# A two-block transformer kernel on one core: B first, square sums folded, low parts in their own turn, GpSimd held back at nine stage starts

## What is computed

```python
def rms_norm(x, g):
    y = x * lax.rsqrt(jnp.mean(x * x, axis=-1, keepdims=True) + EPS)
    return y * g
...
    h = rms_norm(x, ssm_norm)                       # layer 0
    x = x + s5_mixer(h, ...)                        # state space: u = h @ w_in, complex scan, gelu, @ w_glu
    x = x + conv_ffn(rms_norm(x, ffn_norm), ...)
    x = x + sigmoid(rms_norm(x, ple_norm) @ w_gate) * (p @ w_proj)
    k, v = shared_kv(x, ...)                        # rms_norm(x, kv_norm) @ kv_w, then norms of k
    x = x + diff_attention(rms_norm(x, attn_norm), k, v, ...)
    ...                                             # conv_ffn and the gate again
    x = x + even_mixer(rms_norm(x, g0), ...)        # attention over selected keys, pooled windows
    x = x + swiglu(rms_norm(x, g1), w1, w3, w2)
    x = x + odd_mixer(rms_norm(x, g2), ...)         # stick-breaking attention
    x = x + swiglu(rms_norm(x, g3), w1, w3, w2)
```

## Time and profile before

| | us |
|---|---|
| median of 3 runs | 1413.98 (1412.37 to 1414.03) |
| the profiled execution | 1413.15 |
| its span, first to last instruction | 1411.4 |

### The profile page before, as it was taken

How to read it: one execution, slowest core, us unless ns; L and a number is a source line. 1 busy time by engine, 2 the same in 40 slices (tenths; PEclk the granted TensorE clock), 3 DMA queues, 4 the chain that set the end, 5 groups by cost and what they waited for, 6 DMA issues and landing times.

```text
span 1411.4 us, 28128 instructions
## 1 busy us (share of the span) xinstructions
PE 1343.0 (95%) x11090; PEld 1295.0 (92%) x11090; DVE 688.7 (49%) x1174; ACT 687.4 (49%) x961; POOL 1025.2 (73%) x797
## 2 busy tenths in 40 slices
PE   6989999999999779999999959999999999999999
PEld 6878999999999559999999947999999998999999
DVE  7995565555554765555565584311113454311112
ACT  7624544444655675444446445533345444644442
POOL 1225998888778508888887582888887764888885
PEclk9899999999999789999999978999999999999999
DMA  6312555545457304554454430455544433355540
GB/s 252 120 61 104 203 179 180 178 178 182 146 155 227 144 1 150 187 180 178 178 180 148 181 120 9 176 187 186 189 178 157 150 120 120 136 194 179 178 149 30
DMA packets 33878, 217.07 MB, mean 154 GB/s; under 512 B 3683, under 2 KB 7428, under 8 KB 8196
## 3 DMA queue, kind: packets, MB, share of 16 engines
q1 hardware_dynamic: 30096, 211.14, 41.9%
...
...
## 4 chain that ended last, share of the span: by engine, by line
PE 60%; POOL 20%; issue 10%; DVE 7%; ACT 2%; DMA 1%; DVEq 0%; POOLq 0%; SPq 0%; ACTq 0%
POOL w_lo L339 19%; PE up L1331 14%; PE up L1333 13%; PE up L1332 13%; PE acc L1331 5%; PE acc L1333 4%; PE acc L1332 4%; PE side L1338 2%; PE side L1514 1%; PE acc L1487 1%; PE up L1433 1%; DMA mix<-in_s_b 1%; DVE mix L1217 1%; ACT w_hi L401 1%; DVE mix L1114 1%
## 5 line engine op out<-in xcount | busy, mean ns | idle before, releaser
L339 POOL TENSOR_TENSOR w_lo<-ring,w_hi 128x512 fp32r<-128x512 f32 x764 | 988.5, 1326 | 291.8 <-ACT w_hi L401 290.6
L1331 PE MATMUL up<-opnd,w_hi 128*128 128x256 f32 x2208 | 637.5, 289 | 8.5 <-DVE opnd L941 2.0
L1333 PE MATMUL up<-opnd,w_hi 128*128 128x256 f32 x2208 | 624.9, 283 | 0.0
L1332 PE MATMUL up<-opnd,w_lo 128*128 128x256 f32 x2208 | 624.8, 283 | 0.0
L401 ACT ACTIVATE w_hi<-ring 128x2048 fp32r<-128x2048 f32 x193 | 368.2, 1909 | 269.8 <-PE up L1333 215.0
L1331 PEld LDWEIGHTS up<-opnd,w_hi 128*128 128x128 f32 x2208 | 423.7, 192 | 14.9 <-issue 4.4
L1332 PEld LDWEIGHTS up<-opnd,w_lo 128*128 128x128 f32 x2208 | 423.7, 192 | 1.4
L1333 PEld LDWEIGHTS up<-opnd,w_hi 128*128 128x128 f32 x2208 | 423.5, 192 | 0.0
L1331 PE MATMUL acc<-opnd,w_hi 128*128 128x256 f32 x736 | 208.5, 283 | 2.5 <-DVE opnd L1013 2.5
L1332 PE MATMUL acc<-opnd,w_lo 128*128 128x256 f32 x736 | 208.3, 283 | 0.0
L1333 PE MATMUL acc<-opnd,w_hi 128*128 128x256 f32 x736 | 208.3, 283 | 0.0
...
## 6 DMA issues: line engine op xcount, KB each, us to landing
...
```

What stands on the lines that cost most here:

```text
L339: ins = nc.gpsimd.tensor_tensor(w_lo[:, b, cols], ring[:, r, cols], w_hi[:, b, cols].bitcast(f32), ALU.subtract)
L1331: MM(o, l_hi, r_hi, start=start, stop=False, skip_group_check=True)
L1332: MM(o, l_lo, r_hi, start=False, stop=False, skip_group_check=True)
L1333: return MM(o, l_hi, r_lo, start=False, stop=stop, skip_group_check=True)
```

## The change

1. **B first.** SP issues `s5_b` ahead of x and slot 0. ACT makes the compact copies of B first, then the copies of x, then new compact copies of C (`s_cn`), so that all complex products take the compact form; both products of C stand ahead of `evacuate(0)`. `turns(1)` (whole turns of the second table) is DVE's instead of ACT's. PE's transposes of the product of B stand ahead of the square sums.
2. **Square sums folded.** In place of `square_sum` after every k, `square_sums(h)` runs after k=3 and after k=7: four matmuls with 32 columns of ones, each in a column group of its own, so that aux[1] holds 4 x 32 rows of partial sums. ACT copies them out (`ssq_sb`), and one full matmul `all_sums`, after k=0 of the next slot, sums the four groups; ACT then does Ln (its scale has 1/32 in it, as each group's sum stands in 32 rows) and Exp. For token norms `token_rstd`, after k=3 of that next slot, turns `rstd` by two matmuls of one column, and ACT copies the result.
3. **Low parts in their own turn.** In `ple` and `residual` both low tiles of a pair stand after both additions; in `glu` a tile's low part stands right behind its addition. `hi` stands ahead of `sq` on ACT.
4. **GpSimd held back.** `low_parts` is cut at the third slot (START+2) of nine stages, and waits there until the eight low tiles of that stage's operand are made (`lo_ready`). Ranges under 12 slots are written out instead of looped.
5. **End of the state-space stage.** The last two sums (n=7) are DVE's. `s5_out` has its loop over k outermost and waits for each piece of `s5_p`. `w_low(glu+1)` stands behind outputs 6 and 7, `neg_lam` after the low parts. ACT waits for `s5_p` ahead of `s5_act(5)`.

```diff
...
     sp.dma_start(par[:], a["par"]).then_inc(dma["par"], 16)
+    sp.dma_start(s_in[:, 1], a["s5_b"].rearrange("p r m t -> p r (m t)")).then_inc(dma["s5_mat"], 16)
     sp.dma_start(x[:], a["x"]).then_inc(dma["x"], 16)
     load(0, slice(0, 1))
-    sp.dma_start(s_in[:, 1], a["s5_b"].rearrange("p r m t -> p r (m t)")).then_inc(dma["s5_mat"], 16)
     sp.dma_start(s_craw, a["s5_c"]).then_inc(dma["s5_c"], 16)
     for s in range(1, RING - 1):
         load(s, slice(s, s + 1))
...
 
-    for n in range(KT):
+    for n in range(KT - 1):
...
     low_part(first)
 
+    borders = {START[f] + 2: u for f, u in (("ffn0", "ffn0"), ("ple0", "ple0"), ("kvq", "kv"), ("ffn1", "ffn1"),
+                                            ("ple1", "ple1"), ("evin", "even"), ("ffn2", "ffn2"),
+                                            ("qkv", "odd"), ("ffn3", "ffn3"))}
+
     def low_parts(first, end):
+
+        cuts = [first] + [s for s in sorted(borders) if first < s < end] + [end]
+        for a, b in zip(cuts, cuts[1:]):
+            if a in borders:
+                pool.wait_ge(sem("lo_ready"), KT * (UNIT[borders[a]] + 1))
+            steady(a, b)
+
+    def steady(first, end):
+        if end - first < 2 * RING:
+            for s in range(first, end):
+                low_part(s)
+            return
...
     def new_operand(name, squares=True):
 
         for m in range(KT):
+            c.up(A(hi(name)[:, m], x[:, m], ACT.Copy, scale=gain(name, m)), "hi_ready")
             if squares:
                 c.up(A(sq[:, m], x[:, m], ACT.Square), "sq_ready")
-            c.up(A(hi(name)[:, m], x[:, m], ACT.Copy, scale=gain(name, m)), "hi_ready")
 
...
 
         nc.scalar.preload_act_table_set("natural_log_exp_and_others")
         c.wait("ssq")
-        c.up_and_wait(A(rstd[:], aux[1][:, 0:T], ACT.Ln, scale=1.0 / D, bias=eps), "act_step")
+        c.up(A(rstd[:], aux[1][:, 0:T], ACT.Copy), "ssq_sb")
+        c.wait("ssq_all")
+        c.up_and_wait(A(rstd[:], aux[1][:, 0:T], ACT.Ln, scale=1.0 / (QUAD * D), bias=eps), "act_step")
         c.up(A(rstd[:], rstd[:], ACT.Exp, scale=-0.5), "rstd")
         if tokens:
-            c.up_and_wait(A(tok[:, 2:4], aux[0][:, 0:2], ACT.Ln, scale=1.0 / D, bias=eps), "act_step")
-            c.up(A(tok[:, 2:4], tok[:, 2:4], ACT.Exp, scale=-0.5), "rstd_tok")
+            c.wait("tok_ps")
+            c.up(A(tok[:, 2:4], aux[0][:, 0:2], ACT.Copy), "rstd_tok")
...
     c.up(A(w[:, 7], w[:, 4], ACT.Sin, scale=TWO_PI / 2), "s5_sc")
     act.wait_ge(dma["par"], 16)
-    act.wait_ge(dma["x"], 16)
-    for m in range(KT):
-        c.up(A(ssm_x[:, m], x[:, m], ACT.Copy, scale=gain("ssm", m)), "ssm_ready")
...
             c.up(A(own(s_bn, h)[0][:, r], part[:, :, cols], ACT.Copy, scale=1.0 - 2.0 * r), "s5_bn")
+    act.wait_ge(dma["x"], 16)
+    for m in range(KT):
+        c.up(A(ssm_x[:, m], x[:, m], ACT.Copy, scale=gain("ssm", m)), "ssm_ready")
+    act.wait_ge(dma["s5_c"], 16)
+    for h in range(2):
+        part, cols = own(s_craw, h)
+        c.up(A(own(s_cn, h)[0], part[:, :, :, cols], ACT.Copy), "s5_cn")
...
         c.up(A(s_in[:, 0, r], acc[:, 2 * r:2 * r + 2].rearrange("p a b -> p (a b)"), ACT.Copy), "s5_ab_sb")
     act.wait_ge(dma["s5_t"], 16)
-    s5_turns(1)
     act.wait_ge(sem("s5_zero"), 2)
...
         decay(n)
         s5_act(n - 3)
+    act.wait_ge(sem("s5_p"), 3 * KT)
     s5_act(KT - 3)
-    act.wait_ge(sem("s5_p"), 3 * KT)
...
     step(TTo(w[:, 15], w[:, 2], w[:, 3], ALU.add))
     dve.wait_ge(dma["s5_t"], 16)
-    first_turns()
+    turns(0)
     c.wait("s5_clear", 2)
     c.wait("s5_bn", 4)
-    complex_product(s_ab[:, 0], s_ab[:, 1], s_bn, 10, 11, ALU.add, ALU.subtract, "s5_ab", True)
-    dve.wait_ge(dma["s5_c"], 16)
-    complex_product(s5_cm[:, 0, 0], s5_cm[:, 1, 0], s_craw, 12, 13, ALU.subtract, ALU.add, "s5_cm", False)
+    complex_product(s_ab[:, 0], s_ab[:, 1], s_bn, 10, 11, ALU.add, ALU.subtract, "s5_ab")
+    c.wait("s5_cn", 2)
+    complex_product(s5_cm[:, 0, 0], s5_cm[:, 1, 0], s_cn, 12, 13, ALU.subtract, ALU.add, "s5_cm")
+    complex_product(s5_cm[:, 0, 1], s5_cm[:, 1, 1], s_cn, 14, 15, ALU.subtract, ALU.add, "s5_cm")
     c.wait("rstd")
     evacuate(0)
-    complex_product(s5_cm[:, 0, 1], s5_cm[:, 1, 1], s_craw, 14, 15, ALU.subtract, ALU.add, "s5_cm", False)
-    c.wait("lam_exp")
-    step(TTo(neg_lam, little[:, 4:5], little[:, 3:4], ALU.subtract))
-    step(V.tensor_scalar(neg_lam, neg_lam, -LAM_INIT, None, ALU.add))
-    less_whole(1)
+    turns(1)
...
         c.up(TTo(s_m[:, b], sn, bu, ALU.mult), "s5_prod")
 
     def s5_scan(n):
-        c.wait("s5_sum", 2)
+        if n < KT - 1:
+            c.wait("s5_sum", 2)
+        else:
+            z, m = s_z[:, n % 2], s_m[:, n % 2]
+            also(TTo(z[:, 0], z[:, 0], m[:, 1], ALU.add))
...
             s5_output(n - 2)
     s5_low(KT - 3)
-    w_low(START["glu"] + 1)
     s5_output(KT - 2)
     s5_output(KT - 1)
+    w_low(START["glu"] + 1)
     s5_low(KT - 2)
     s5_low(KT - 1)
+    c.wait("lam_exp")
+    step(TTo(neg_lam, little[:, 4:5], little[:, 3:4], ALU.subtract))
+    step(V.tensor_scalar(neg_lam, neg_lam, -LAM_INIT, None, ALU.add))
...
         c.tell("up_free")
         c.up_and_wait(V.tensor_tensor(x[:, m], x[:, m], f_h[:, 0], ALU.add), "x_ready")
-        if m:
-            low_tile("ffn0", m - 1)
-    low_tile("ffn0", KT - 1)
+        low_tile("ffn0", m)
...
                 c.up_and_wait(V.tensor_tensor(x[:, m], x[:, m], f_c[:, b + e], ALU.add), "x_ready")
-                if m:
-                    low_tile(ends[0], m - 1)
-        low_tile(ends[0], KT - 1)
+            for e in range(2):
+                low_tile(ends[0], 2 * g + e)
...
         return MM(o, l_hi, r_lo, start=False, stop=stop, skip_group_check=True)
 
-    def square_sum(k, tokens):
-
-        c.wait("sq_ready")
-        ins = MM(aux[1][:, 0:T], ones, sq[:, k], start=(k == 0), stop=(k == KT - 1), skip_group_check=True)
-        if tokens:
-            for t in range(TT):
-                ins = MM(aux[0][:, t:t + 1], sq[:, k, t * P:(t + 1) * P], ones[:, 0:1],
-                         start=(k == 0 and t == 0), stop=(k == KT - 1), skip_group_check=True)
-        if k == KT - 1:
+    def square_sums(h):
+
+        c.wait("sq_ready", KT // 2)
+        for q in range(4):
+            ins = MM(aux[1][QUAD * q:QUAD * q + QUAD, 0:T], ones[:, 0:QUAD], sq[:, 4 * h + q],
+                     start=(h == 0), stop=(h == 1), tile_position=(0, QUAD * q), skip_group_check=True)
+        if h:
             c.up(ins, "ssq")
...
+    def all_sums():
+
+        c.wait("ssq_sb")
+        c.up(MM(aux[1][:, 0:T], ones, rstd[:], start=True, stop=True, skip_group_check=True), "ssq_all")
+
+    def token_rstd(norms):
+
+        c.wait("rstd", norms)
+        for t in range(TT):
+            ins = MM(aux[0][:, t:t + 1], rstd[:, t * P:(t + 1) * P], ident[:, 0:1],
+                     start=(t == 0), stop=(t == TT - 1), skip_group_check=True)
+        c.up(ins, "tok_ps")
+
+    def between(k, fold, tokens):
+
+        if fold and k == 0:
+            all_sums()
+        if tokens and k == 3:
+            token_rstd(tokens)
...
                 ins = three(o[:, m], w_hi[:, b, w], w_lo[:, b, w], hi(name)[:, k], lo(name)[:, k],
                             k == 0 and m == 0, k == KT - 1)
-            if sums and k < KT - 1:
-                square_sum(k, False)
+            if sums and k == KT // 2 - 1:
+                square_sums(0)
+            between(k, fold, tokens)
         c.up(ins, "mm_done")
         if sums:
-            square_sum(KT - 1, False)
+            square_sums(1)
...
     s5_transposed(lambda r, m: s_in[:, 1, r, m * P:(m + 1) * P], "s5_bt_ps")
     o = whole_bank(S)
     whole_part(S, o, range(KT), fresh=True)
-    for m in range(KT):
-        square_sum(m, False)
     c.wait("s5_ab", 4)
     c.wait("s5_bt", 2)
     s5_transposed(lambda r, m: s_ab[:, r, 4 * m:4 * m + 4].rearrange("p a b -> p (a b)"), "s5_ab_ps")
+    for h in range(2):
+        square_sums(h)
+    all_sums()
...
                 MM(bank(i)[:, 0:P], s_k0[:, 2 * M + i], sq[:, 2 * M + i, 0:P], start=(i == 0), stop=False,
                    skip_group_check=True)
-        c.wait("s5_p", 3)
-        for i in range(2):
-            for k, v in enumerate((s_pc[:, n % 2, 0], s_pc[:, n % 2, 1], s_ps[:, n % 2, 1],
-                                   s_ps[:, n % 2, 0])):
+        for k, v in enumerate((s_pc[:, n % 2, 0], s_pc[:, n % 2, 1], s_ps[:, n % 2, 0], s_ps[:, n % 2, 1])):
+            if k != 1:
+                c.wait("s5_p")
+            r = k if k < 2 else 3 - k
+            for i in range(2):
...
-    token_slot("kv", S + 1)
+    token_slot("kv", S + 1, fold=True, tokens=4)
...
                                 first, last)
-            if i == 0 and k < KT - 1:
-                square_sum(k, True)
+            between(k, i == 1, 2 if i == 1 else 0)
         if half:
             c.up(ins, "mm_done")
-            if i == 0:
-                square_sum(KT - 1, True)
```

(2 more changed lines are left out.)

49 lines of the change are left out of this document (22 added, 27 removed).

## The result

The changed kernel took **1400.34 us** (median of 4 runs, 1398.24 to 1401.01) against 1413.74 for the kernel before (1412.37 to 1414.03): ratio 0.9902, 95% interval 0.9887 to 0.9918. The forecast was 1409 with a range from 1386 to 1418, and faster at 0.70. Run a second time beside other kernels, the same kernel gave 1403.32 (1399.44 to 1404.72), ratio 0.992 (0.9903 to 0.9936); the eight runs together have the median 1401.0. Two things above have to be set right. The stages have 197 slots, of which the 193 from `glu` on go through ACT and POOL as described. And `s5_out` of one n uses two of the four column groups (q is 2b or 2b+1 in its code), not all four; the other two are the next n's.

The account below looks back on a forecast made before the run. PE, busy for 95% of the span, was taken as the bound. Terms -5.6 - 3.3 + 0.4 - 0.2 + 0 - 1.9 = -10.6, with the clock -5.0, gave 1408.2, as median 1409; range 1386 to 1418.

Parts of the forecast that it names:

- Narrow sums and fold: PE's square sums: eight narrow sums 1.1, fold 0.45, wait 0.25; a plain norm 1.8 in place of 3.2.
- The four ffn norms: Plain norms of the four ffn stages: 1.4 less each, -5.6 together.
- The rival that switches to column groups cost much: PE around narrow sums: four switches in each of nine norms drain it, +6 to +11, 1415 to 1420; chance 0.05.
- `ple` into a token norm: First slot of `kvq` and `evin`: DVE's low tile k=6 comes late, PE waits 3.5 (2.8 to 4.9).
- The fold behind it: Second slot of `kvq` and `evin`: PE waits for ACT's copy, 2.9 (1 to 4) and 2.3 (0.5 to 3.7).
- The clock: Behind pauses at `kvq` and `evin`: PE's clock halves for a while, 2.8 a place, +5.6 (0 to 10).
- `qkv`: Token norm at `qkv`: -4.6, with 1.3 back (0 to 2.5) as the fold waits for ACT; together -3.3.
- The start: Start of the state-space stage: first scan input between 37 and 42, gain lost at `evacuate(0)`; 0 (-3 to +2).
- The end of the stage: End of the state-space stage: last two sums on DVE save 0.9, `s5_out` and low parts 1.0; -1.9 (-3 to 0).
- The hold: GpSimd held back: costs nothing (0 to +1 a place); without it `kvq` would wait 2 more.
- DVE did not keep up: Rival: DVE under 5.8 a group from `ple` on, neither pause nor clock loss, -24.1, 1387 to 1390; chance 0.25.
- the pauses did not each cost 5: Rival: every pause halves the clock, full 5 at `kvq`, `evin` and the start, 1417 to 1421; chance 0.12.

Follow-up runs that it names:

- experiment 8: Changed kernel with first two slots of `kvq` and `evin` interleaved, first fold later, first norm's copy ahead of table load, `ple` low tiles one behind: 1398.54 us.
- experiment 4: Changed kernel with low tiles one behind again in `glu`, `ple` and `residual`: 1401.78 us, ratio 0.9929.
- experiment 9: Changed kernel with first fold later, first norm's copy ahead of table load, plus absolute value of the logits on ACT instead of DVE: 1394.43 us.
- experiments 2 and 7: 2: parts 1 and 5 alone on the kernel before, 1407.81 us; 7: changed kernel, first fold later, first norm's copy ahead of table load, 1398.52 us.
- experiment 3: Changed kernel without part 4, GpSimd not held: 1406.66 us, ratio 0.9959.
- experiments 1 and 2: 1: part 2 alone on the kernel before, 1405.65 us; 2: parts 1 and 5 alone on the kernel before, 1407.81 us.

## Why the prediction was right, and where its sizes were off

- **Narrow sums and fold.** Eight sums were put at 1.1 and cost 1.4; with the fold a plain norm was put at 1.8 and cost 1.9 in `ffn1` to `ffn3` (the first four slots took 24.97 instead of 26.42) and 2.5 in `ffn0`. The four ffn norms gave -5.2 where -5.6 was forecast (0.9 in `ffn0`, 1.45 in each other). The row that the 1.1 came from was read wrongly, and the price was near by luck: the 64 records of `s5_out` have 127 columns to stream where the wide ones have 256, and they use two column groups at a time, not four. Half the length and half the groups cancel. The rival that switches to column groups cost much falls: the ordinary slots beside the sums kept their 5.76. Around a group of four there are 0.78 us from the matmul before it to the one behind, 0.12 of which is that matmul's own turn, so 0.66, where four quarters of 0.46 give 0.46. What the Trainium skill calls a drain ("TensorEngine Tiling (Array Packing)", Key Properties) would fit these 0.2, but no run here separates it from the weight loads of the four groups.
- **`ple` into a token norm.** Counted from the end of the first gate slot (364.51), DVE's fourth group began at 21.56 (forecast 21.8), tile 6's low part was there at 25.7 (26.3), and PE waited 2.8 (3.5). This step was right: the cover was gone. (A small slip in its working: by the earlier trace rows the first two of the ten low tiles end near 397.1, not 397.9, if they run alike, so the lower bound of a group is 6.1 and not 6.3.)
- **The fold behind it** was put at 2.9 and 2.3 and cost 0.6 and nothing. This step failed, twice over. ACT's copy came 0.9 earlier than forecast, since the squares ended at 26.2 and not 27.0. And PE arrived at the fold 1.4 later, though its pause had ended 0.4 earlier, because tiles 6 and 7, the sums and the next tile ran at half clock: the loss to the clock and the wait for ACT lie over each other, while the sum added them.
- **The clock** was charged 2.8 a place; it was 3.41 us at half speed, 1.7 of loss, at each. The prediction took this from one stretch of 10.1 us and put the border between a pause of 1.96 and one of 2.60. That border didn't hold: pauses of 2.0 were followed by half clock in `kvq` in experiment 8 and in `evin` in experiment 4, 2.95 in `evin` in experiment 9 by none. Forecast for both places together, pauses, folds and clock: +5.8; the table has -0.6 and -1.5 for the steps with the gate slots and norms in them. That is 7.9 of the 8.4 between forecast and result; the state-space stage gave 2.1 more than forecast, and the attention stretches took 2.0 back.
- **`qkv`** was put at -3.3 and gave -3.7 (the table's -5.1 less `ffn2`'s 1.4).
- **The start** was put at 0. The whole change had `rstd` at 32.76 (forecast 32.7) and the first input at 39.05 (37 to 42), but the reason given was wrong: `evacuate(0)` doesn't eat what B first brings. Alone, parts 1 and 5 give -5.2; it is the fold ahead of slot 1 that takes back 3 us of the first input's start, as PE stood still for 2.2 behind ACT's tables and then ran 3.41 us at half clock (experiments 2 and 7). The step that failed is that the fold was costed only where a next slot hides it; at the start it had none.
- **The end of the stage** was put at -1.9; the last scan came 1.1 sooner after the one before, and PE resumed `glu` 1.2 sooner after it: -2.2.
- **The hold** was rightly free for POOL, and put at 2 for `kvq` by the low tiles. Measured 3.9 in all with the product out of the way. Shared between the two places that is 2 each, but the pauses have only 0.65 each of it, and in `kvq` in experiment 3 the fold's wait took that up. The term was right in size and its reason was partly wrong: most of it is half clock, which differs between executions.
- **The attention stretches** were left at nothing and gave -1.7, +1.5 and +2.2. In the last of them PE's pause of 2.49 in `out`, for POOL's `w_lo`, was followed by half clock, where two pauses of 1.18 and 1.84 before had none. It isn't the hold's, as it is there without the hold too (experiment 3). In the second the 3.4 us more at half clock would be 1.7 of loss, an estimate; the first stays unexplained.

Of the rivals, none came: DVE did not keep up, and the pauses did not each cost 5. The forecast of 1409 was right in direction for the reason given, PE's time for the square sums; that it was 8 too high comes from terms that were added and overlap. The sum of experiments 1 and 2, -12.6, is near the change's gain, but not a proof that nothing else counts: the hold's 3.9 (not in either) and the 3 that the fold takes at the start (in neither) go against each other; whether the order of the low tiles has any share of its own stays open.
